# Front of a hybrid layer: the u projection as seven half-size block products, all input tiles loaded at once

## The reference, cut to what matters

```python
h = _rmsnorm(x, w["g_mix"])
proj = h @ w["w_in"]                       # (1088 x 1024) @ (1024 x 1536)
u_s5 = proj[..., :D_S5]                    # 512 columns: this is "u"
x_lru = proj[..., D_S5:D_S5 + D_LRU]       # 512 columns
g_lru = proj[..., D_S5 + D_LRU:]           # 512 columns
```

## Time and profile before

| | |
|---|---|
| median of the three runs | 1156.3 us |
| the profiled execution's own time | 1158.44 us |
| its span in the profile | 1156.3 us |
| mean granted clock of TensorE | 0.991 of full speed |
| busy: PE, DVE, ACT | 1105.2 us (96%), 620.9 us (54%), 246.7 us (21%) |
| HBM read, written | 187.05 MB, 28.53 MB |

### The profile page before, as it was taken

The page is one execution under the profiler, slowest core; times in us unless marked ns, Lnnn a source line. Parts: engine busy times, 40 slices in busy tenths (PEclk is TensorE's granted clock), DMA queues, the critical chain, the costliest instruction groups (busy, mean ns, idle before and its releaser), DMA issues.

```text
span 1156.3 us, 15254 instructions
## 1 busy us (share of the span) xinstructions
PE 1105.2 (96%) x6175; PEld 622.5 (54%) x6175; DVE 620.9 (54%) x1217; ACT 246.7 (21%) x528; POOL 80.7 (7%) x108
## 2 busy tenths in 40 slices
PE   5999999999999999999999999999899999999975
PEld 3666766678765444788766645555433333333322
DVE  4575599927857566733376686667512121211127
ACT  4300321355641001100033211011111111110115
POOL 5000010101000000000000000000212111121010
PEclk9999999999999999999999999999999999999998
DMA  9009460177461003200244540046589999999639
GB/s 308 28 1 203 44 41 1 55 207 279 151 267 23 0 1 125 94 1 1 76 179 148 181 182 38 36 138 254 202 338 416 415 416 417 410 403 406 234 134 386
DMA packets 65367, 209.26 MB, mean 181 GB/s; under 512 B 13560, under 2 KB 22416, under 8 KB 57072
## 3 DMA queue, kind: packets, MB, share of 16 engines
q1 hardware_dynamic: 54528, 177.68, 43.5%
q0 software_dynamic: 10640, 30.55, 7.5%
q10 hardware_dynamic: 128, 0.03, 0.0%
HBM read 187.05 MB, written 28.53 MB: 186 GB/s over the span
## 4 chain that ended last, share of the span: by engine, by line
PE 83%; DMA 8%; DVE 5%; issue 2%; ACT 1%; SPq 0%; DVEq 0%; POOLq 0%; ACTq 0%
PE bank L691 16%; PE bank L1209 11%; PE bank L854 9%; PE bank L919 8%; PE bank L1226 6%; PE bank L1049 6%; DMA arena<-in_w_down 6%; PE bank L663 5%; PE bank L813 3%; PE bank L951 2%; PE bank L1016 2%; PE bank L1197 2%; PE bank L780 1%; DMA arena<-in_w_in 1%; PE bank L961 1%
## 5 line engine op out<-in xcount | busy, mean ns | idle before, releaser
L691 PE MATMUL bank<-arena 128*128 128x360 f32 (+1 forms) x576 | 181.0, 475 | 2.7 <-DMA arena<-in_w_in 2.6
L1209 PE MATMUL bank<-arena 128*32 128x512 f32 x1536 | 170.0, 594 | 1.0 <-DVE arena L2296 1.0
L691 PEld LDWEIGHTS bank<-arena 128*128 128x128 f32 x576 | 110.2, 193 | 68.3 <-issue 3.3
L1916 DVE TENSOR_TENSOR arena<-arena,bank 128x512 f32<-128x512 f32 (+3 forms) x56 | 68.4, 1221 | 66.8 <-PE bank L919 37.4
L1209 PEld LDWEIGHTS bank<-arena 128*32 128x32 f32 x1536 | 47.4, 110 | 105.2 <-issue 103.9
L854 PE MATMUL bank<-arena 128*128 128x272 f32 x448 | 103.0, 392 | 0.0
L1049 PE MATMUL bank<-arena 128*128 128x512 f32 x224 | 100.6, 598 | 0.2 <-DVE arena L2081 0.2
L919 PE MATMUL bank<-arena 128*128 128x512 f32 x224 | 97.7, 593 | 0.0
L1226 PE MATMUL bank<-arena 128*32 128x512 f32 x768 | 88.3, 601 | 6.4 <-DMA arena<-in_w_down 5.8
L854 PEld LDWEIGHTS bank<-arena 128*128 128x128 f32 x448 | 85.0, 190 | 17.4
L2300 DVE TENSOR_TENSOR arena<-arena,bank 128x256 f32<-128x256 f32 x24 | 10.1, 421 | 156.6 <-ACT arena L1508 156.6
(11 more groups left out here) (409 smaller groups left out, 1337.1 us busy)
## 6 DMA issues: line engine op xcount, KB each, us to landing
arena<-in_w_gate SPq DMA_DIRECT2D x32, 1024.0 KB
arena<-in_w_up SPq DMA_DIRECT2D x32, 1024.0 KB
arena<-in_w_down SPq DMA_DIRECT2D x32, 1024.0 KB, 14.0
arena<-in_ck SPq DMA_DIRECT2D x8, 1024.0 KB, 7.6
arena<-in_cv SPq DMA_DIRECT2D x8, 1024.0 KB, 5.8
arena<-work_moe SPq DMA_DIRECT2D x16, 512.0 KB, 10.9
arena<-in_w_in SPq DMA_DIRECT2D x3, 2048.0 KB, 15.0
arena<-in_x SPq DMA_DIRECT2D x8, 512.0 KB, 7.5
```

The lines of the kernel that those rows point to most:

```text
L691: last = nc.tensor.matmul(b[:, 0:w], win[slot][:, k, m * P:m * P + P], ht[:, k, c0:c0 + w], start=k == 0, stop=k == KD - 1)
L1209: last = nc.tensor.matmul(bank[2 + j % 2][t0:t0 + QT, :].rearrange("p (h n) -> p h n", h=2), xgt[j % 2][:, k, t0:t0 + QT], gu[e % GUB][:, ...
L1916: V.tensor_tensor(out, out, bank[banks(n)][:, :].unsqueeze(1).to_broadcast([P, width, 512]), ADD).then_inc(sem["md_free"], 1)
```

## The change

**u as a 2 x 2 block product.** The weights of u are cut into four blocks of 512 features x 256 columns (a11, a12, a21, a22), `ht` into four blocks of 512 features x 544 tokens (b11, b12, b21, b22), and u into four blocks of 256 columns x 544 tokens. Instead of eight block products there are seven, of sums of blocks; DVE forms four sums of weight blocks (us1 to us4, 128 x 1024 each) and four of token blocks (ut1 to ut4, 128 x 2176 each), and adds the seven products together.
- A block product is four "fills" of one bank (`u_fill`): 128 output columns x 272 tokens, four matmuls each. So there are 28 fills, in place of 12 groups of eight matmuls.
- Eight fills go to the MA ring and are drained by ACT (`u_copy`); twenty go to a ring of four other banks (`u_ring`, banks 4, 5, 7, 6) and are added straight from the bank by DVE (`u_own`, `u_m6`, `u_m57`, `u_m4`).
- The twenty fills count on the semaphores q_full, q_free and q_sum, whose later users get an offset (`U_FILLS`, `U_SUMS`).

**Loads.** Each tile has a slot of its own; SP issues all of them without a wait. The three small loads for the angles are issued ahead of the weights of u, and the weights of x_lru after tile 7 is transposed.

**Order.** On PE the tiles 3 to 8 are transposed between the first eight fills, the four small transpose fills come after 22 of the 28 fills, and the gnat fills one group later. On DVE the angles come ahead of tile 3, tiles 3 to 8 in one run, then the sums; the S5 scalars are cut apart by `u_m57`.

The diff, cut to its core:

```diff
@@ SP
             def load_x(n):
-                if n >= XR:
-                    sp.wait_ge(sem["tp_full"], tile_fills(n - XR))
-                sp.dma_start(xst[n % XR][0:ROWS[n], :], ...)
+                sp.dma_start(xst[n][0:ROWS[n], :], ...)
...
-            load_win(0, 0)
-            load_x(3)
             for src, dst in ((I["lam_re"], ...), (I["lam_im"], ...), (I["log_dt"], ...)):
                 sp.dma_start(dst, src).then_inc(sem["lam_in"], 16)
-            for n in range(4, 6):
+            load_win(0, 0)
+            for n in range(3, NT):
                 load_x(n)
+            sp.wait_ge(sem["tp_full"], tile_fills(7))
             load_win(1, DH)
-            for n in range(6, NT):
-                load_x(n)
-
-            sp.wait_ge(sem["ma_free"], MA_U)
+            sp.wait_ge(sem["q_free"], U_FILLS)
             sp.dma_start(W["u"]..., ut[:, :, :]).then_inc(sem["u_out"], 16)
@@ PE
-            project(0, 0, 1, 0, norm_after(3, 0))
-            project(0, 0, 1, 1, norm_after(6, 1))
+            def u_ring():
+                n = un.next()
+                if n >= 4:
+                    pe.wait_ge(sem["q_free"], n - 3)
+                return bank[UB[n % 4]]
+
+            def u_fill(b, a_, b_, q, done):
+                m, n = UQ[q]
+                for k in range(4):
+                    last = nc.tensor.matmul(b[:, 0:UN], a_[:, k, P * m:P * m + P], b_[:, k, UN * n:UN * n + UN], start=k == 0, stop=k == 3)
+                last.then_inc(sem[done], 1)
...
+            m1(0)
+            m1(1)
+            m2(0)
+            norm_t(3)
+            m2(1)
+            for n in range(4, 6):
+                norm_t(n)
+            pe.wait_ge(sem["tp_free"], tile_fills(4))
+            m1(2)
+            norm_t(6)
+            m1(3)
+            norm_t(7)
+            m2(2)
+            norm_t(8)
+            m2(3)
+            pe.wait_ge(sem["q_sum"], 3)
+            pe.wait_ge(sem["tp_free"], tile_fills(8))
+            for q in range(4):
+                u_fill(claim(MA, ma, "ma_free"), us4, b22, q, "ma_full")
+            pe.wait_ge(sem["q_sum"], 6)
+            for q in range(4):
+                u_fill(u_ring(), us2, ut2, q, "q_full")
+            for q in range(3):
+                u_fill(u_ring(), us1, ut1, q, "q_full")
+                pe.wait_ge(sem["q_sum"], 7)
+                u_fill(u_ring(), us3, ut3, q, "q_full")
 
             pe.wait_ge(sem["scal_ok"], 1)
...
-            project(0, 0, 1, 2)
-
-            project(1, 1, 1, 0, gnat_after(0, 2))
-            project(1, 1, 1, 1, gnat_after(1, 1))
+            u_fill(u_ring(), us1, ut1, 3, "q_full")
+            u_fill(u_ring(), us3, ut3, 3, "q_full")
+            pe.wait_ge(sem["q_sum"], 8)
+            for q in range(4):
+                u_fill(u_ring(), a22, ut4, q, "q_full")
+
+            project(1, 1, 1, 0, gnat_after({3: (0, 0)}))
+            project(1, 1, 1, 1, gnat_after({0: (0, 2), 2: (1, 0), 3: (1, 2)}))
+            pe.wait_ge(sem["q_free"], U_FILLS)
@@ ACT
-            for n in range(4):
+            for n in range(3):
                 square(n)
             act.wait_ge(sem["lam_in"], 48)
...
+            link(nc.scalar.activation(warm[:, :], zero1[:, 1:2], ACT.Sqrt))
+            for n in range(3, 6):
                 square(n)
-            drain_u(0, 0)
+            u_copy(1, 1, 0)
+            u_copy(1, 1, 1)
+            for n in range(6, NT):
+                square(n)
+            u_copy(1, 1, 2)
+            u_copy(1, 1, 3)
             act.wait_ge(sem["ang_ok"], 1)
...
+            for q in range(4):
+                u_copy(0, 1, q)
@@ DVE
-            xn(3)
...
+            dve.wait_ge(sem["win_in0"], 16)
+            u_ready(V.tensor_tensor(us1[:, :, :], a21, a22, ADD))
+            xn(3)
+            u_ready(V.tensor_tensor(us2[:, :, :], us1[:, :, :], a11, SUB))
             xn(4)
             evac(3)
             xn(5)
             evac(4)
+            xn(6)
             evac(5)
+            xn(7)
+            evac(6)
+            u_ready(V.tensor_tensor(us4[:, :, :], a12, us2[:, :, :], SUB))
+            xn(8)
+            evac(7)
+            evac(8)
+            dve.wait_ge(sem["tp_free"], tile_fills(8))
+            u_ready(V.tensor_tensor(us3, a11, us3, SUB))
+            u_ready(V.tensor_tensor(ut1[:, :, :], b12, b11, SUB))
+            u_ready(V.tensor_tensor(ut2[:, :, :], b22, ut1[:, :, :], SUB))
...
+            def u_m57(q):
+                c12, c21, c22 = u_part(0, 1, q), u_part(1, 0, q), u_part(1, 1, q)
+                b5 = u_next()
+                dve.wait_ge(sem["ma_free"], 4 + q + 1)
+                link(V.tensor_tensor(c12, c12, b5, ADD))
+                b7 = u_next()
+                link(V.tensor_tensor(c21, c22, b7, ADD), V.tensor_tensor(c12, c12, c22, ADD))
+                V.tensor_tensor(c22, c21, b5, ADD).then_inc(sem["q_free"], 2)
...
+            for n in range(4):
+                u_own(n)
+            u_ready(V.tensor_tensor(ut3[:, :, :], b22, b12, SUB))
+            for n in range(4):
+                u_m6(n)
+            u_ready(V.tensor_tensor(ut4[:, :, :], ut2[:, :, :], b21, SUB))
+            u_m57(0)
             dve.wait_ge(sem["trig_ok"], 3)
...             (the first run of the S5 scalars)
+            u_m57(1)
...             (the second run, ending in scal_ok)
-            tiles(6, NT)
+            u_m57(2)
...             (copies out of the small transpose fills)
+            u_m57(3)
...             (pw and bbar)
+            for n in range(4):
+                u_m4(n)
...             (hmat, gnat)
```

More of the change, by code:

```diff
@@ L116, in hybrid_layer @@
         win = [reg(a, KD, 512) for a in (R_WA, R_WB)]
-        XR = 4
-        xst = [reg(R_XL + 1024 * s, D) for s in range(XR)]
+        XSLOT = [R_XL + 1024 * s for s in range(4)] + [R_WB + 1024 * s for s in range(4)] + [R_UC]
+        xst = [reg(a, D) for a in XSLOT]
+        x_in = [f"x_in{n}" if n < 4 else f"f_in{n - 4}" for n in range(NT)]
         memr = [reg(R_TMP + 288 + 1024 * s, D) for s in range(MT)]
@@ L166, in tile_fills, with u_part, u_bank @@
             return 2 * (n + 1)
-        HT_READY = [tile_fills((c0 + w - 1) // P) for c0, w in CHUNKS]
+        UH, UN, UK = TOK // 2, TOK // 4, TOK // 4 // L
+        UQ = [(0, 0), (1, 0), (0, 1), (1, 1)]
+        UB = (4, 5, 7, 6)
+        U_FILLS, U_SUMS = 20, 8
+        us1, us2, us4 = (reg(R_G + 1024 * (s + 1), 4, 256) for s in range(3))
+        us3 = win[0][:, 0:4, 256:512]
+        ut1, ut2, ut3, ut4 = (reg(a, 4, UH) for a in (R_GL, R_GL + 4 * UH, R_UC, R_UC + 4 * UH))
+        def u_part(row, col, q):
+            m, n = UQ[q]
+            k0 = UK * (2 * col + n)
+            return ut[:, 2 * row + m, :].rearrange("p (t k) -> p t k", t=L)[:, :, k0:k0 + UK]
+        def u_bank(b):
+            return bank[b][:, 0:UN].rearrange("p (k t) -> p t k", t=L)
         G_TP0 = tile_fills(NT - 1) + 4
@@ L300, in hybrid_layer @@
         fdg = reg(R_R, len(FPE), 2, P)
-        FIN = [(f"f_in{i}", 32) if i < 6 else (f"x_res{i - 6}", 48) for i in range(NT)]
+        FIN = [(f"f_in{i}", 32 + 16 * (i < 5)) if i < 6 else (f"x_res{i - 6}", 48) for i in range(NT)]
         gfin, squaresf = reg(18432, D), reg(19456, D)
@@ L1303, in square @@
                 r = ROWS[n]
-                act.wait_ge(sem[f"x_in{n % XR}"], 16 * (n // XR + 1))
-                link(nc.scalar.activation(squares[0:r, :], xst[n % XR][0:r, :], ACT.Square, accum_out=ssq[0:r, n:n + 1]))
+                act.wait_ge(sem[x_in[n]], 16)
+                link(nc.scalar.activation(squares[0:r, :], xst[n][0:r, :], ACT.Square, accum_out=ssq[0:r, n:n + 1]))
                 nc.scalar.activation(rstd[0:r, n:n + 1], ssq[0:r, n:n + 1], ACT.Sqrt, scale=1.0 / D, bias=zero1[0:r, 1:2]).then_inc(sem["std_ok"], 1)
@@ L1311, in drain, with u_copy @@
                 nc.scalar.activation(out, bank[ring[n % 2]][0:out.shape[0], 0:w] if isinstance(w, int) else w(bank[ring[n % 2]]), func, **kw).then_inc(sem[free], 1)
[L1313 to L1316, removed]
+            def u_copy(row, col, q):
+                n = ma.next()
+                act.wait_ge(sem["ma_full"], n + 1)
+                nc.scalar.activation(u_part(row, col, q), u_bank(MA[n % 2]), ACT.Copy).then_inc(sem["ma_free"], 1)
             def drain_x(ci, m):
@@ L1657, in _, with u_next, u_own, u_m6 @@
             evac(4)
+            xn(6)
             evac(5)
+            xn(7)
[8 more added lines that the diff above has]
+            u_ready(V.tensor_tensor(ut2[:, :, :], b22, ut1[:, :, :], SUB))
+            uf = Count()
+            def u_next():
+                n = uf.next()
+                dve.wait_ge(sem["q_full"], n + 1)
+                return u_bank(UB[n % 4])
+            def u_own(q):
+                b = u_next()
+                dve.wait_ge(sem["ma_free"], q + 1)
+                V.tensor_tensor(u_part(0, 0, q), u_part(1, 1, q), b, ADD).then_inc(sem["q_free"], 1)
+            def u_m6(q):
+                b = u_next()
```

(10 more changed lines are left out.)

88 lines of the change are left out of this document (42 added, 46 removed).

## The result

| | before | after |
|---|---|---|
| median of the runs | 1156.3 us | 1163.59 us (1163.09 to 1166.56, five runs) |
| the profiled execution's own time | 1158.44 us | 1164.36 us |
| its span, mean granted clock | 1156.3 us, 0.991 | 1162.6 us, 0.984 |

After to before is 1.007, with an interval of 1.0049 to 1.009: slower by 7.3 us between the medians, by 8.1 us (5.7 to 10.4) by the ratio. The forecast was 1163.2 us.

A forecast was written before the change was run, and what follows sets the result against it. PE bounds the kernel; its 7.0 us saving is spent waiting for DVE. Start 0.4, gnat stall 4.8 and half clock 1.7 give about +6.9 on 1156.3, so 1163.2 us; range 1156.0 to 1168.0.

The forecast's parts named there:

- PE still sets the pace: Rival, faster: DVE in time at scal_ok and gnat, gain 6.6 us, 1149.7 us; chance 0.12.
- The clock holds: Rival, no measurable difference: clock stays up at both stalls, leaving +3.4 us, 1159.7 us; chance 0.22.
- Stepped reads cost DVE: Rival, slower still: DVE's adds from banks take 0.65 us each, 3.1 us more, 1166.3 us; chance 0.17.
- The weights land late: Rival, slower: all 2.7 us of small-load issue delays the start instead of 0.4, +9.2 us, 1165.5 us; chance 0.04.
- Steps 6 and 7: Last six fills and x_lru groups, then gnat: half clock costs 1.8 and 1.7 us; PE stands 4.8 us for gnat.
- DVE almost without idle from 40 us on: Sign that the forecast is right, to be seen on DVE in the front of the kernel.
- Stepped reads with a late landing: Upper end of the range, 1168.0 us: slow DVE adds from banks together with a late landing of the weights.
- step 3: Products us4 b22 and us2 ut2: PE to 55.7 us; on DVE u_own to 47.7, u_m6 to 56.3, ut4 to 58.7.
- What DVE gains in work: Work added to DVE, all before gnat: weight sums 4.9 us, token sums 9.7, 28 adds 12.3; together 27 us.
- Step 4: Six fills of us1 ut1 and us3 ut3 bring PE to 66.7 us; scal_ok at 73.3, so PE stands 6.6 us.
- Reaches the end whole: Behind the lag products: the shift of about +6.9 us is carried to the end of the kernel undiminished.

The follow-up runs named there:

- the scalars early: The changed kernel with nine steps of the S5 scalars between the four u_m6 and the other fifteen behind u_m57(1): 1161.58 us, ratio 1.005 to the kernel before.
- gnat later: The changed kernel with the first gnat fills asked for one projection group later again, the others behind it: 1158.31 us, ratio 1.0018 to the kernel before.
- the new order: The change with 28 fills in one PE run, scalars spread over DVE's pauses, gnat later: 1151.27 us, ratio 0.9957 to the kernel before.
- the clock kept up: The changed kernel with unread filler matmuls on PE, seven before the scal_ok wait, five before the first gnat fill: 1160.69 us, ratio 1.004 to the kernel before.
- the loads alone: The kernel before with only the change's loads (nine slots, reordered issue), products of u as before: 1156.28 us, ratio 0.9999 to the kernel before.

## Why the prediction was right

The mechanism was forecast: two waits of PE for DVE at the two named places, of nearly the forecast lengths, each with a half clock behind it. Step by step, predicted and measured on the profiled execution:

| step | predicted | measured |
|---|---|---|
| 1 PE starts | 19.4 | 19.21 |
| 2 eight fills and all tiles | 41.1 | 41.5 (39.67 + one fill) |
| 4 PE reaches the first wait | 66.7 | 67.44 |
| 4 `scal_ok`; PE stands | 73.3; 6.6 | 73.87; 6.49 |
| 5 small fills done | 76.9 | 77.48 |
| 6 last fills; four groups | 89.7; 109.5 | 88.95; 108.9 |
| 7 gnat ready; PE stands | 114.3; 4.8 | 113.27; 4.42 |
| 6 half clock behind the first wait, in the fills | 1.8 | 0.6 |
| 7 half clock behind the second wait | 1.7 | 3.1 |
| lag products against before | +6.9 | +7.4 |

- **The rivals.** "PE still sets the pace" fell by both waits. "The clock holds" fell by the stretches at 0.50. "Stepped reads cost DVE" fell by the adds: 0.44 us alone, and four in a row in 1.48 us; the upper bound of 0.65 was not needed. So the lines of 8 bytes that the Trainium skill gives for PSUM (SBUF — State Buffer, "Door 1: The DMA port swizzle") cost DVE's stepped reads nothing here. DVE's sums took 0.44 us for 272 elements, 1.23 for 1024 and 2.42 for 2176. The Trainium skill, VectorE: DVE Perf Modes, section "The TRN2 errata", gives (N + 151) / 0.96 ns for an f32 add of two tensors; worked out for these sizes, that is an estimate of 0.44, 1.22 and 2.42 us. The traces agree with all three, also where one operand is a stepped bank. "The weights land late" fell by 19.21.
- **Steps 6 and 7, the half clock.** The prediction had 3.5 us for both, this execution 3.7, but shared out otherwise. In this execution the half clock behind the second wait cost 0.93 (1.97 against 1.04 for eight transposes) and 2.13 (7.14 against 5.01): 3.1 us, not 1.7. Behind the first wait the six fills took 11.63 against 11.04, 0.6 us in place of 1.8; the small transposes ran slowly there too, but they have to wait for DVE in any case. The two errors nearly cancel. Other executions had it as forecast. These are two lines of the kernel without ut4, whose waits are 6.49 and 4.43 us:

```profile
77.61 12.79 PE L735 MATMUL bank<-arena 128*128 128x272 f32 x48
...
116.03 6.20 PE L694 MATMUL bank<-arena 128*128 128x360 f32 x16
```

  The six fills took 12.79, 12.64, 12.92 and 13.01 us in the kernels without ut4, without ut3, with the scalars early (a first wait of 3.96 us) and with gnat later: 1.6 to 2.0 us lost, near the 1.8 of step 6. Behind the second wait, of 4.40 to 4.43 us in the first three of these, 1.8 us were lost each time (1.62 + 6.20, 1.77 + 6.05 and 1.48 + 6.34 against 1.04 + 5.01). The second loss thus differed by 1.3 us behind waits of the same length, and one profile does not give its size.
- **Luck in the 0.4 us.** The forecast is off by 0.4 us, and that is better than its parts. PE came to the second wait at 108.9, 0.2 us ahead of the 109.1 of the kernel before and not 0.4 behind it, and waited 0.4 less; the clock took 1.4 more. And the profile that all of it was added to had lost some 1.6 us to the half clock itself (last section). The mechanism is shown by the waits and the runs, and not by the closeness of the number.
- **A sign that was wrong.** "DVE almost without idle from 40 us on" did not come: from 40.00 to 113.27 DVE is busy for 62.31 us of 73.27. The prediction's own schedule had these pauses ("some 10 us"), and the kernels with the scalars early and with the new order show that they could be used.
- **A bound.** Stepped reads with a late landing add up to 1163.2 + 3.1 + 2.3 = 1168.6, above the 1168.0 at which the range ends. Nothing hangs on it here.
- **Mis-sized, step 3.** The eight adds of `u_own` and `u_m4` take 1.48 a four, not 1.8.
- **A cause that does not hold.** "What DVE gains in work" counts 27 us as if each microsecond pressed on the same chain. The chain to `scal_ok` begins at the fill behind `u_m57(0)`, near 60 us; the sums ahead of it lie in pauses. Step 4 had it so ("needs the fill that ends at 59.4"), yet I then expected 2.4 us from taking ut4 away. What decided was the order: scalars behind `u_m57`, and gnat asked for at a fixed group. The kernel in another order shows it, with the same added work still there and both waits gone. No run takes away the first wait alone; one shortens it by 2.5 us.
- **The sum at the end.** The shift of 7.4 us at the lag products is 6.3 us at the end of the span and 7.3 between the medians. "Reaches the end whole" holds within the spread of the runs; the two single executions differ in the experts' stage, where the shift is 8.0 us at 823 us and 5.5 at the last matmuls, and the cause stays open.

## What to carry to other kernels

When a change takes work from the bounding engine and gives work to a second one, sum the second one's chain from its last forced wait to each point where the first asks for it, not its total. Work that fits into the pause ahead of that wait was free here (ut3, ut4); work behind it set when PE's wait ended. Then look for the order before giving up the change. Here the same arithmetic took 1163.6 us with two waits of 6.5 and 4.4 us, and 1151.3 with none over 0.51.

## What the runs showed of the hardware that I had not expected

- The granted clock in the profile can read 1.00 where the records run at the pace of the half clock. These are stretches of 2 us just after PE's start, from the kernel after and from the one with the clock kept up:

```profile
21.00:23.00 2.00, 2.00 (x6) 1.52 (x5) 0.29 (x2) 1.68 (x4) 0.00 (x0) 0.50 1.03 410
```

```profile
21.00:23.00 2.00, 2.00 (x6) 1.53 (x5) 0.00 (x0) 1.51 (x4) 0.00 (x0) 1.00 1.04 414
```

  Both have six records in 2 us, at 0.50 in one and at 1.00 in the other; the same fills at full rate have ten or eleven in each of the stretches from 66 to 74 us of the reordered kernel. So durations are to be trusted over that column. What held the records up at 1.00, no view shows; a DMA share over 1 stands in both.
- The first 24 records behind the landing of the weights took 7.25 to 8.55 us in seven executions of the same instructions, 5.5 at full rate. That start moves everything behind it, and is a good part of why one profile can't settle 1 us.
- The kernel before lost some 1.6 us at half clock behind its small transposes in its profiled execution (0.50; 112 records in 35.97 us in PE's timeline, 35.77 in the chain). In the kernel with the loads alone the same waits of 0.36 and 0.69 us were followed by 112 records in 34.37 us of the timeline, and the granted clock reads 1.00 from 66 to 74 us. So the same short waits cost 1.6 us in one execution and nothing in the other.
